# A fused encoder step with 32 experts: the last two pairs' rows added by a 0/1 product, the others read back earlier

## The reference, cut to what matters

```python
h = _rmsnorm(x, norm1_g) * (1.0 + sc1) + sh1
...
x = x + g1 * (mix @ w_out)
h2 = _rmsnorm(x, norm2_g) * (1.0 + sc2) + sh2
x = x + g2 * _hier_moe(h2, w_rg, b_rg, w_re, b_re, w1, w3, w2)

# _hier_moe: top-1 of 4 groups, then top-2 of that group's 8 experts
gate = jnp.sum(jax.nn.one_hot(eid, N_EXPERTS) * top_w[..., None], axis=1)
hid = jax.nn.silu(jnp.einsum('nd,edf->nef', hf, w1)) * jnp.einsum('nd,edf->nef', hf, w3)
hid = hid * gate[..., None]
y = jnp.einsum('nef,efd->nd', hid, w2)
```

## Time and profile before

| what | value |
|---|---|
| median of 3 runs | 802.78 us (801.38 to 804.58) |
| the profiled execution's own time | 803.89 us |
| span of the profile | 802.1 us |
| mean granted TensorE clock | 0.956 |
| PE busy | 688.2 us (86%) |
| DVE, ACT, POOL busy | 351.5, 270.2, 94.8 us |
| DMA traffic | 199.17 MB, mean 248 GB/s |

### The profile page before, as it was taken

The page is one execution under the profiler, slowest core; times in us unless marked ns, Lnnn a source line. Parts: engine busy times, 40 slices in busy tenths (PEclk is TensorE's granted clock), DMA queues, the critical chain, the costliest instruction groups (busy, mean ns, idle before and its releaser), DMA issues.

```text
span 802.1 us, 13782 instructions
## 1 busy us (share of the span) xinstructions
PE 688.2 (86%) x5313; PEld 557.0 (69%) x5313; DVE 351.5 (44%) x552; ACT 270.2 (34%) x500; POOL 94.8 (12%) x158
## 2 busy tenths in 40 slices
PE   0698999998799999999988999877999997787760
PEld 0287889987689999999978999755555554444430
DVE  1565677777343433344423356552334232322225
ACT  0444466654443444555334543300111110101010
POOL 2002132222000011111110000001121221111010
PEclk9988999999899999999999999878999999999995
DMA  9958277864636786432216438798999999999925
GB/s 315 356 142 248 86 235 236 249 225 136 210 105 176 182 289 167 122 108 82 84 32 181 133 115 305 256 398 329 418 416 417 417 419 417 417 418 417 390 87 196
DMA packets 131176, 199.17 MB, mean 248 GB/s; under 512 B 11688, under 2 KB 113464, under 8 KB 117816
## 3 DMA queue, kind: packets, MB, share of 16 engines
q1 hardware_dynamic: 123032, 185.63, 65.1%
q0 software_dynamic: 6208, 11.02, 4.0%
q10 hardware_dynamic: 1888, 1.86, 0.8%
HBM read 193.47 MB, written 16.55 MB: 262 GB/s over the span
## 4 chain that ended last, share of the span: by engine, by line
PE 47%; SPq 16%; DMA 9%; DVE 8%; ACT 8%; issue 7%; DVEq 2%; ACTq 2%; POOL 1%; POOLq 0%
PE ps L586 20%; SPq L507 10%; PE ps L581 8%; PE ps L583 8%; PE ps L582 8%; SPq L517 5%; DMA e_w<-in_w 4%; DMA ada_first<-in_w_ada 4%; ACT w_hi L1138 4%; DVE w_lo L1453 2%; DVE w_lo L1463 1%; DMA yb<-expert_rows 1%; ACT sig_r L1257 1%; ACT probs L1238 1%; ACT z_na L1303 1%
## 5 line engine op out<-in xcount | busy, mean ns | idle before, releaser
L586 PE MATMUL ps<-e_w,xgT 128*64 128x256 f32 x1024 | 116.8, 384 | 18.9 <-DMA e_w<-in_w 11.0
L586 PEld LDWEIGHTS ps<-e_w,xgT 128*64 128x64 f32 x1024 | 76.5, 138 | 54.6 <-DMA e_w<-in_w 14.1
L581 PE MATMUL ps<-hT_hi,w_hi 128*128 128x320 f32 x320 | 102.3, 320 | 4.5 <-DVE w_lo L1453 4.2
L1453 DVE TENSOR_TENSOR w_lo<-raw,w_hi 128x2048 fp32r<-128x2048 f32 (+1 forms) x26 | 68.1, 2619 | 81.2 <-ACT w_hi L1138 81.2
L583 PE MATMUL ps<-hT_hi,w_lo 128*128 128x320 f32 x320 | 99.6, 311 | 0.0
L582 PE MATMUL ps<-hT_lo,w_hi 128*128 128x320 f32 x320 | 99.4, 311 | 0.0
L586 PE MATMUL ps<-e_w,hidT 128*64 128x512 f32 x256 | 58.5, 598 | 10.9 <-issue 10.0
L581 PEld LDWEIGHTS ps<-hT_hi,w_hi 128*128 128x128 f32 x320 | 60.7, 190 | 7.2 <-issue 4.1
L1798 DVE TENSOR_SCALAR h_s<-h_e 128x256 f32<-128x256 f32 x16 | 4.7, 295 | 136.2 <-ACT h_e L1370 136.2
L1138 ACT ACTIVATE w_hi<-raw 128x2048 fp32r<-128x2048 f32 (+1 forms) x26 | 56.4, 2170 | 21.7 <-PE ps L583 21.7
L582 PEld LDWEIGHTS ps<-hT_lo,w_hi 128*128 128x128 f32 x320 | 60.7, 190 | 0.0
(11 more groups left out here) (260 smaller groups left out, 1260.2 us busy)
## 6 DMA issues: line engine op xcount, KB each, us to landing
e_w<-in_w SPq DMA_DIRECT2D x96, 1024.0 KB, 24.2
raw<-in_w_in SPq DMA_DIRECT2D x45, 512.0 KB
ada_late<-in_w_ada SPq DMA_DIRECT2D x16, 1024.0 KB, 7.2
ada_first<-in_w_ada SPq DMA_DIRECT2D x8, 1024.0 KB, 21.6
raw<-in_w_in SPq DMA_DIRECT2D x8, 1024.0 KB
raw<-in_w_oa SPq DMA_DIRECT2D x4, 1024.0 KB
raw<-in_w_ob SPq DMA_DIRECT2D x4, 1024.0 KB
raw<-in_w_out SPq DMA_DIRECT2D x4, 1024.0 KB
```

Of the source, the lines that this page charges most:

```text
L581: nc.tensor.matmul(out, lhs_hi, rhs_hi, start=first, stop=False, skip_group_check=True)
L586: return nc.tensor.matmul(out, lhs, rhs, start=first, stop=last, skip_group_check=True)
L1453: V.tensor_tensor(w_lo[j][:, :, 0:width], raw[j][:, :, 0:width], f32(w_hi[j][:, :, 0:width]), ALU.subtract).then_inc(split_done, 1)
```

## The change

- GpSimd scatters only the first 14 pairs (`SENT = PAIRS - 2`). It then waits for these and at once issues the loads of `ya` and `yb`, in the layout of five half rows (the sample's 64 rows folded over 128 partitions), and two of `g2_fold`. GpSimd, no longer DVE, adds `ya` and `yb`.
- Since rows of pairs 14 and 15 are never written, SP fills `y_dram` with zeros by five transfers of 512 KB during the first attention.
- The rows of pairs 14 and 15 stay on chip. DVE compares each slot's token number with a row of column numbers (`select`), a 0/1 matrix of slots by tokens. DVE scales the output of `down` by routing weight and g2 (`gated`, once for each sequence), and PE multiplies matrix and rows into banks 0 to 4 (`add_rows`). DVE adds these sums to `x_out`, which holds `x + g2 * (ya + yb)` of the other pairs (`part`).
- `ya`, `yb`, `x_out` and `g2_fold` lie in the ring slot of pair 13, which is slot 1, also that of pair 1. For later rounds, `load_up` of pair 1 therefore waits on `y_done`, in every round, at `TILES * r + 2`. DVE adds 2 to `y_done` ahead of its loop over rounds.
- The next round's slot table is made at pair 8 instead of after pair 15, through `R_next`.
- `h_s` goes: `swiglu` works in `h_e` and `hid`. ACT makes one copy of half the sample's rows ahead of its loop. Some semaphores are joined.

```diff
+SENT = PAIRS - 2
...
+        zero_rows = place("zero_rows", [P, D // 4], F32, (end - D) // 32 * 32)
...
+        back_at = ew_at + (SENT - 1) % RING * ring_pair
+        ya, yb, x_out = (place(n, [P, 5, HALF], F32, back_at + 20 * HALF * j) for j, n in enumerate(("ya", "yb", "x_out")))
...
+            sp.wait_ge(setup_done, 3)
+            for n in range(2 * TOK // P):
+                sp.dma_start(y_dram[1 + n * P:1 + (n + 1) * P].rearrange("p (b n) -> p b n", b=4),
+                             zero_rows[:].unsqueeze(1).broadcast_to([P, 4, D // 4])).then_inc(late_moves, 16)
...
                 if p == RING - 1:
                     sp.wait_ge(h2_ready, 3)
+                if p == (SENT - 1) % RING:
+                    done = sp.to_reg(TILES * r + 2)
+                    sp.wait_ge(small_in, 16)
+                    sp.wait_ge(y_done, done)
+                    sp.free_register(done)
...
+            def add_rows(r, n):
+                yp, ys = y_sb[n], xg[1 + n]
+                steps = (((0, 0, 0), (0, 1, 1), (1, 0, 2), (1, 1, 3)), ((0, 0, 0), (1, 0, 2), (0, 1, 1), (1, 1, 3)))[n]
+                for i, (t, half, b) in enumerate(steps):
...
+                    last = mm(ps[:, b, :], sel[n][:, t * P:(t + 1) * P], yp[:, half * HALF:(half + 1) * HALF], n == 0, n == 1)
+                    if n and half:
+                        last.then_inc(oh_out, 1)
...
+                for half in range(2):
+                    last = mm(ps[DEC * half:DEC * (half + 1), 4, :], sel[n][:, SEQ:TOK], ys[:, half * HALF:(half + 1) * HALF],
+                              n == 0, n == 1)
...
+                    if p == PAIRS // 2:
+                        slot_table(r + 1, (R_next[:], R_next[:]))
+                add_rows(r, 0)
                 down(r, PAIRS - 1)
-                slot_table(r + 1)
+                add_rows(r, 1)
...
+            for _ in range(2):
+                dve.nop().then_inc(y_done, 1)
+            dve.wait_ge(g2_in, 16)
             with dve.Fori(0, rounds) as r:
...
+                for n, p in enumerate((SENT, SENT + 1)):
+                    dve.wait_ge(e_y, PAIRS * r + p + 3)
+                    dve.wait_ge(y_stored[n], 16 * (SENT // 2) * (r + 1) + 16)
+                    if n == 0:
+                        gated(y_sb[0][:], 0, p, slice(0, 2)).then_inc(oh_in, 1)
+                    else:
+                        for half in range(2):
+                            gated(y_sb[1][:], 0, p, slice(half, half + 1)).then_inc(oh_in, 1)
+                    gated(xg[1 + n][:], 1, p, slice(0, 2)).then_inc(oh_in, 1)
+                    dve.drain()
+                    dve.nop().then_inc(e_yv, 1)
+                    if n == 0:
+                        for t in range(TILES):
+                            part(r, t)
+                        dve.drain()
+                for t in range(TILES):
+                    dve.wait_ge(oh_out, TILES * r + t + 1)
+                    V.tensor_tensor(shaped(columns_of(x_out, t), t), added[t], shaped(columns_of(x_out, t), t), ALU.add).then_inc(y_done, 1)
...
-                for p in range(PAIRS):
+                for p in range(SENT):
...
+                for t in range(TILES):
...
+                    pool.wait_ge(back[t], landed)
+                    G.tensor_tensor(ya[:, cols, :], ya[:, cols, :], yb[:, cols, :], ALU.add).then_inc(y_sum, 1)
```

More of the change, by code:

```diff
@@ L65, in shape_constants @@
     late[:, L_FOLD:L_FOLD + 36] = (r[:, None] % 64 == np.arange(36)[None, :])
+    late[:, L_COL:L_COL + P] = np.arange(P)
     for n in range(2):
@@ L233, in build @@
         h_e = [take(f"h_e{j}", [P, FE]) for j in range(2)]
-        h_s = [take(f"h_s{j}", [P, FE]) for j in range(2)]
         late_cst = take("late_cst", [P, L_ALL])
+        R_next = take("R_next", [P, TILES, P])
+        tok = take("tok", [P, TILES, 2])
         assert cursor[0] <= lam_end
@@ L563, in _ @@
                 sp.reg_load(count, rnd_i[0:1, 0:1])
[L564 to L569, removed]
+            rounds = sp.value_load(rnd_i[0:1, 0:1], min_val=1, max_val=MAX_ROUNDS)
+            for t in range(TILES):
+                done = sp.to_reg(TILES * rounds + t)
+                sp.wait_ge(small_in, 16)
+                sp.wait_ge(y_done, done)
+                sp.free_register(done)
+                if t < 2:
+                    sp.dma_start(t_out["y_prompt"][t * P:(t + 1) * P], x_out[:, 2 * t:2 * t + 2, :].rearrange("p b n -> p (b n)")).then_inc(stored, 16)
+                else:
+                    for half in range(2):
+                        sp.dma_start(t_out["y_sample"][:, half * HALF:(half + 1) * HALF], x_out[DEC * half:DEC * (half + 1), 4, :]).then_inc(stored, 16)
+            sp.wait_ge(stored, 64)
             for s in a_stored + b_stored:
@@ new lines, in select, with gated, banks @@
+            def select(n):
+                for t in range(TILES):
+                    w = rows_of(t)
+                    V.tensor_scalar(sel[n][:, t * P:t * P + w], late_cst[:, L_COL:L_COL + w], tok[:, t, n:n + 1], None, ALU.is_equal)
+            def gated(out, sequence, p, halves):
+                def banks(a):
+                    return a.rearrange("p (b n) -> p b n", b=2)[:, halves, :]
+                return V.scalar_tensor_tensor(banks(out), ps[:, 5 + halves.start:5 + halves.stop, :], row_w[:, p:p + 1],
+                                              banks(g2b[:, sequence, :]), ALU.mult, ALU.mult)
@@ L1821, in _ @@
                     last = V.tensor_copy(row_w[c, :], own[:, 2, :])
+                    owned.append((c, own))
                 dve.drain()
                 dve.nop().then_inc(tab_ready, 1)
+                for c, own in owned:
+                    for t in range(TILES):
+                        V.tensor_scalar(tok[c, t, :], own[:, 0, SENT:PAIRS], float(NO_ROW - t * P), None, ALU.add)
                 columns_out(r, 0)
@@ L1899, in _ @@
                 rope(m, m, None)
+            pool.wait_ge(ada_used, KD)
+            G.memset(zero_rows[:], 0.0)
+            pool.drain()
+            pool.nop().then_inc(setup_done, 1)
             with pool.Fori(1, 4) as i:
@@ L1974, in scatter @@
                                      y_sb[j][:], None, bounds_check=2 * TOK, oob_is_err=False).then_inc(y_stored[j], 16)
-                pool.free_register(n2)
-                pool.free_register(before)
+                for v in (n2, n3, before):
+                    pool.free_register(v)
             with pool.Fori(0, rounds) as r:
```

178 lines of the change are left out of this document (116 added, 62 removed).

## The result

The change runs in **818.89 us** (median of 4 runs, 817.72 to 820.69), the kernel before beside it in 802.08 us (4 runs, 798.12 to 804.58): ratio **1.0241**, 95% interval 1.0211 to 1.0271. The medians are 16.8 us apart; the ratio, which is not their quotient, stands for 19.3 us (16.9 to 21.7). The forecast was 812 us in a range of 804 to 818: the sign and the main cause are right, the size is 7 us short, and the median lies 0.9 us outside the range. The profiled execution took 817.94 us, with a span of 816.2 us.

A forecast was written before the change was run, and what follows sets the result against it. The weight stream was taken to bound the experts, its last landing starting the tail. The wait's +15 us less the tail's 5.5 gave +9.5 on the 802.78 us median: 812 us, range 804 to 818.

The forecast's parts named there:

- The wait, +15 on L: SP's wait on y_done ahead of pair 1 delays eight weight transfers; 14.1 to 15.8 us, taken as +15 us.
- L: The moment the last weight transfer lands and the tail starts; 772.1 us in the kernel before, 30.0 us before the end.
- Zeros, 0 (bound 2): Five 512 KB zero transfers during attention: taken as 0, at most 2 us if a weight unit were late.
- step 1: The wait on y_done ahead of pair 1, with all of SP's queue behind the waiting instruction: +15 us.
- Pair 8's slot table: Some 3 us of work moved from behind pair 15 to pair 8, within the weight stream's slack: 0.
- The tail, L+24.5: End 24.5 us after the last weight landing against 30.0, gaining 5.5; L+23.2 at full clock, L+26.5 at half, bound L+28.
- The sum: Late start and tail together: +15 - 5.5 = +9.5 us, forecast 812 us.
- Rival A: The forecast itself: late weight start and a middling tail, +5 to +13 us, 808 to 816; chance 0.64.
- C: Tail gives nothing back: held-up read-backs, half-clock PE, late sums, shared interfaces; +13 to +16 us, 816 to 819; chance 0.17.
- B: The weight stream catches up with late pair 1, only the tail changes: 797 us, down to 792; chance 0.07.
- D: Small stall and a quick tail: +14 - 10.5 = +3.5 us, 806; chance 0.12.
- The last rival: Read-backs don't run beside the last weights because their write-out lands too late; 5 us of overlap, C's upper end.

The follow-up runs named there:

- e12: e2, but DVE gives its two counts behind its last copies ahead of the router, a 7.0 us wait: 804.50 us, ratio 1.0030 to the kernel before.
- e1: The kernel before with only the wait on y_done ahead of pair 1's weights and the two counts ahead of DVE's loop: 815.71 us, ratio 1.0146.
- e13: e11 with the two counts given late, ahead of DVE's expert loop, as in the change: 812.44 us, ratio 1.0119 to the kernel before.
- e2: The changed kernel with the two counts of y_done given at the start of DVE's program: 803.10 us, ratio 1.0019 to the kernel before.
- e9: e2 with the five zero transfers issued by GpSimd behind its last rope step, not by SP: 799.77 us, ratio 0.9987 to the kernel before.
- e7: e2 with the read-backs issued only when the last weights have landed: 805.07 us, ratio 1.0067 to the kernel before.
- e5: e2 with pair 15's scaled rows ahead of the second and third part on DVE: 799.42 us, ratio 0.9984 to the kernel before.
- e11: e2 with e9's zeros, e5's order, g2_fold loaded before the write-out wait, sums on GpSimd: 796.82 us, ratio 0.9938 to the kernel before.
- e10: As e11, but sums on DVE and only the sample's part behind pair 15's scaled rows: 797.54 us, ratio 0.9943 to the kernel before.

## Why the prediction was right or wrong

Executions of one kernel differ by up to 8 us in their times (797.94 to 806.20 for the kernel before, beside e12); the terms are measured in the traces, one execution each.

1. *The wait, +15 on L*: right. 538.7 us for the issue, DMA engines empty until then, L moved by 15.1 us in e1 and by 16 in e13. By the ratios the wait is 11.7 us in e1, 14.5 in e13 and 17.8 between e2 and the change, each good to 3 to 4 us. That the gather's wait gives back part of it is also right: e12's 7 us cost nothing that can be seen. No run takes the later first gather by itself; e1's 15.1 us leave no room for it.
2. *Zeros, 0 (bound 2)*: **wrong, about 4 us** in the traces (2.6 by the ratio of e9). The step looked at bytes beside DMA slack, and at a late weight unit. It did not count the five issues on SP and the stores queued behind them, for which ACT waits, though step 1 says that all of SP's queue stands behind one instruction. The trace of before had a nearby price: the weight issue at 152.26 above takes 1.14 us, so five would have been 5.7 us on SP; they took 7.3.
3. *Pair 8's slot table*: 0 fits, though no run takes it alone: wait and zeros, 15.1 and 4.0, already make up the 18.5 us on L, and in e9, which has the table at pair 8, L is 0.6 us later than before.
4. *The tail, L+24.5*: **wrong, L+28.7**, at its own bound of L+28 or just outside it. Three of its steps were short. The read-backs began at L-4.7, not L-6.6, since write-out 13 was issued at L-14.0 and took 8.7 us, where the step had L-15.1 and 7.9. Tile 1 landed at L+8, not L+6, only because of that start: from the first issue it took 12.7 us, and the forecast 12.6. Tile 0 came at L+2.6, the step's late bound, but after 7.4 us, between the 5.5 of idle engines and the 9.2 of that bound. DVE's instruction beside GpSimd's sum took 2.27 us instead of 1.22. So pair 15's first product came at L+16.5 instead of L+13.5; and it ran at half clock, as the text's upper value of L+26.5 had it, so that DVE's last addition ended at L+25.1. Those 3 us on top of 26.5 give 29.5, near what was measured; the forecast took a value between the clocks where the pause alone spoke for the lower.
5. *The sum*: 15 + 4 - 1.4 = 17.6 us by the traces, where the forecast had 15 + 0 - 5.5 = 9.5. The 8.1 us between them are zeros and tail in about equal parts, each good to 1 or 2 us; the medians have 16.8, the ratio 19.3.

Rival A was taken for likeliest. C is nearest to what came, and that its 816 to 819 us hold the 818.89 is in part luck: C put the whole excess into the tail and nothing into the zeros, which cost 4 us. Its mechanisms are all in the trace: late read-backs, half clock, and the shared interfaces, the last with 1.05 us in one instruction where C had 2 to 3 us. The sentence of the Trainium skill (GPSIMD Engine Reference, Specifications), that GpSimd's SBUF interfaces are shared with DVE where DVE has two SBUF inputs, agrees with the trace, 2.27 us for 1.22 and 3.36 for 1.23. That 1 us belonged in the main sum and not in a rival. B fell with e1. D had a quick tail, L+19.5, which no run with the change's order shows. The last rival, that write-out 13 lands too late for the read-backs to run beside the last weights, is half true: it landed at L-5.3 and not at L-7.2, and by e7 the early start still wins 3 us.

Two things were not tried: tokens in a second round, which the wait is there for, and the tail with TensorE kept busy to the end. So how much of the tail's 4 us is the half clock and how much the late start stays an account from the traces; only the order of DVE's work was tested by itself (e5).

## What to carry to other kernels

A wait for a later pass of a loop must be met in the first pass long before the waiting queue gets there; put its opening counts at the start of the engine's program, since everything behind the wait pays, less what a later wait on the same queue had already cost. Cost an added transfer by its issue on the queue and by what stands behind it, before its bytes. In a tail, order an engine's work so that what another engine waits for goes first: here that won 2.8 us, good to 2.4, with the same instructions.

## What the hardware did that was not expected

- A DVE sum or product of 128x1024 from two SBUF operands takes 1.23 us alone, and 2.27 (the change) and 3.36 (e11) beside a sum on GpSimd. GpSimd's two sums beside the 3.36 took 4.56 us instead of 3.57. The two look as if they took turns: in both cases DVE's time is, to 0.13 us, what was left of the GpSimd sum at its start plus its own 1.22. No run separates this from other explanations.
- A 512 KB transfer whose source is one short row read four times takes SP 1.5 us to issue (7.27 us for five, 1.24 to 1.80 each), the same on GpSimd 0.74 (3.71 us for five, e9).
- TensorE's granted clock fell to 0.50, its lower level of 1.2 GHz, behind a pause of 6.4 us in the tail, and it stayed at 1.00 through one of 0.97 (e5). In between, a pause of some 2 us went either way: ahead of `down(14)` the clock stayed at 1.00 before and in e5, and was 0.68 on average, part of the time at the lower level, in the change, e1 and e2; ahead of pair 15's products in e10 a pause of 2.10 us was followed by 0.68. The windows of the kernel after (columns as above), and then of e5:

```profile
804.00:806.00 2.00, 1.92 (x3) 0.92 (x4) 1.78 (x2) 0.00 (x0) 0.00 (x0) 0.50 0.00 0
```

```profile
782.50:786.20 3.70, 3.67 (x10) 1.51 (x12) 3.49 (x3) 0.00 (x0) 2.66 (x2) 1.00 0.00 0
```
